# Grouping the modulation blocks that TensorE sums inside the layers of a two-network kernel

## The chip, the cores and the metric

The kernel runs on one core of a Trainium2 chip. The metric is the device time of one execution in microseconds, as the median of several runs. All times below are from the kernel's runs and from one profiled execution of it.

## What is computed

Two small networks run one after the other on 256 tokens of 2048 channels. Each has two layers, and each layer scales, shifts and gates its input by a modulation vector that comes from a conditioning vector and a large matrix. Cut to what matters here:

```python
def first_block(x, c, norm_g, w_ada, b_ada, w_in, ...):
    c_act = silu(c)
    for l in range(2):
        mod = c_act @ w_ada[l] + b_ada[l]          # (2048) @ (2048, 6144)
        shift, scale, gate = split(mod, 3)
        h = rmsnorm(x, norm_g[l]) * (1 + scale) + shift
        z = h @ w_in[l]                            # (256, 2048) @ (2048, 13 * 512)
        # four mixers on the 13 pieces of z: Fourier, neighbourhood attention,
        # retention, convolution; each times silu of its gate piece
        y = concat(mixers) @ w_out[l]              # (256, 2048) @ (2048, 2048)
        x = x + gate * y
    return rmsnorm(x, final_g)

def second_block(x, c, ctx, c_ctx, ada_w, ada_b, ...):   # a pool layer, then a latent attention layer
    for i in range(2):
        shift, scale, gate = split(silu(c) @ ada_w[i] + ada_b[i], 3)
        shift_c, scale_c, gate_c = split(silu(c_ctx) @ ada_w[i] + ada_b[i], 3)
        ...
```

The four modulation matrices (`ada_w` in the kernel, 50 MB each in float32) are read once, in blocks of 128 rows by 1024 columns, 512 KB each. 16 such blocks, one per 128 rows, make one piece of 1024 modulation values.

## The kernel before, in words

**Slots and steps.** Every large weight matrix comes in slots of 128 x 1024 values. SyncE loads a slot into `w_raw`, ScalarE copies it into `wh` (L1604), VectorE makes the remainder `wl` (L2413), and TensorE does three float32r products with it (`mm3`, L821 to L823). `w_raw`, `wh` and `wl` are rings of `RING = 4` slots: ScalarE may write slot g only when TensorE has used slot g-4 (`w_used`), and SyncE may load into it when VectorE has made `wl` of slot g-4 (`w_lo`). Four slots make a step t; a layer has `STEPS = 35` steps: 26 of the input product, one of two small products, eight of the output product. At the start of a step TensorE does what the mixers need of it (`mixers`), then the four slots i = 0 to 3. Ahead of slots 1, 2 and 3 it calls `ada_middle(t, i)`.

**Modulation blocks.** While the layers of the first network run, 192 blocks of later modulation pieces are summed. `ADA_DVE` and `ADA_PE` list how many blocks of which piece each step takes on VectorE and on TensorE; `ada_schedule()` turns both into one order, `ADA_SEQ`, in which the blocks of a step on the two engines alternate, VectorE's first. GpSimd issues the loads of `ADA_SEQ` strictly in that order (`ada_load`, L761), into a ring of `ADA_RING_A = 4` buffers (three of `ada_raw` and `ada_fourth`): the load of block q first waits until block q-4 has been used, by `ada_pe` if TensorE used it and by `ada_used` if VectorE did. VectorE uses a block in `ada_in_layer` by one multiply-add of 128 x 1024 (L2306), in the steps 8 to 25 mostly right after `wl` of the step's fourth slot. TensorE uses a block in `ada_slot` (L877): four float32 products with a 32-column operand, one for each quarter of the array's columns, which the profile shows as eight matmuls; then `ada_pe` rises by one. TensorE waits for the block's landing (`ada_here(q)`) just ahead of it.

**Where TensorE takes them.** In `ada_middle` a step with one or two TensorE blocks takes them all ahead of its third slot (i = 2). A step with three or four takes the first two ahead of the second slot (i = 1) and the others ahead of the fourth (i = 3). `ADA_PE` gives three blocks or four to 20 of the 46 steps that have any:

```python
ADA_PE = [{**spread(2, 4, [1, 2, 2, 2, 3, 3, 3]), **spread(4, 12, [4] + [3] * 4), **spread(5, 19, [2] * 8)},
          {**spread(2, 2, [2, 2, 2, 2, 2, 3, 3]), **spread(3, 11, [3] * 4 + [2] * 2), **spread(4, 18, [3] * 2 + [2] * 5),
           **spread(5, 26, [3, 4, 1, 2, 3, 3])}]
```

So in the first layer these are the steps 8, 9, 10 and 12 to 16 (step 12 has four blocks), in the second layer the steps 7, 8, 11 to 14, 18, 19, 26, 27, 30 and 31 (step 27 has four). No step with a finished piece (`ADA_FIN`) has three.

Of the kernel before, what the change touches and what calls it, by code (L numbers as in the profile page):

```python
# [107 lines left out]
ADA_FIN = [{11: 2, 17: 4, 18: 0, 27: 5, 28: 1, 34: 3}, {9: 2, 10: 0, 17: 3, 25: 4, 28: 1, 32: 5}]  # L108
# [11 lines left out]
def ada_schedule():  # L120

    slots, pe, dve, done = [], ADA_EARLY, 0, {}
    for l in range(DEPTH):
        for t in range(STEPS):
            if t in ADA_FIN[l] and ADA_FIN[l][t] in ADA_SUMMED[l]:
                pe += 1
                done[l, t] = pe
            elif t in ADA_FIN[l]:
                done[l, t] = pe
            a, b = (x[l].get(t, []) for x in (ADA_DVE, ADA_PE))  # L130
            for i in range(max(len(a), len(b))):
                if i < len(a):
                    dve += 1
                    slots.append((l, t, *a[i], False, dve))
                if i < len(b):
                    pe += 1
                    slots.append((l, t, *b[i], True, pe))
    return slots, done


ADA_SEQ, ADA_DONE = ada_schedule()
# [7 lines left out]
def ada_event(l, t):  # L149

    return 4 + l * 6 + sorted(ADA_FIN[l]).index(t)
# [157 lines left out]
def program(nc, x, w_in, w_small, w_out, ada_w, cols_d, rel_d, tab_d, ctx_in, pool_in, pool_grp, pool_out, mla_in,  # L309
# [4 lines left out]
    with ExitStack() as ctx:  # L314
# [220 lines left out]
        def ada_buf(r):  # L535
            return ada_raw[:, r, :] if r < ADA_RING else ada_fourth[:, :]

        def ada_here(q):

            if q < len(ADA_SEQ):  # L540
                return ada_landed[q % ADA_RING_A], 16 * (q // ADA_RING_A + 1)
            m = q - len(ADA_SEQ)
            return ada_landed[m % ADA_RING], 16 * (len(ADA_SEQ) // ADA_RING_A + m // ADA_RING + 1)
# [274 lines left out]
        def _(pe):  # L818
# [55 lines left out]
            def ada_slot(buf, k, bank_, first=0, last=ADA_SLOTS - 1):  # L874

                for q in range(4):
                    mm = pe.matmul(ps[32 * q:32 * q + 32, bank_, 0:256], cpad[:, k, :], buf[:, q * 256:(q + 1) * 256],  # L877
                                   start=k == first, stop=k == last, tile_position=(0, 32 * q),
                                   skip_group_check=True)
                mm.then_inc(ada_pe, 1)  # L880
# [9 lines left out]
            def ada_turn(event, bank_):  # L890

                pe.wait_ge(ada_row, event + 5 if event else 1)
                for h in range(2):
                    mm = pe.transpose(ps[:, bank_, 256 + h * P:256 + (h + 1) * P], ada_rows[:, h * P:(h + 1) * P], ident)
                mm.then_inc(ada_cols, 1)
# [33 lines left out]
            for l in range(DEPTH):  # L929
# [144 lines left out]
                def ada_middle(t, i):  # L1074

                    if i == 2 and t in ADA_FIN[l]:
                        ada_turn(ada_event(l, t), ADA_FIN_BANKS[l][t])
                    here = sum(x[4] and x[0:2] == (l, t) for x in ADA_SEQ)
                    seen = 0
                    for q, (layer, step, j, k, by_pe, _) in enumerate(ADA_SEQ):  # L1080
                        if by_pe and (layer, step) == (l, t):
                            seen += 1
                            if i != (2 if here < 3 else 1 if seen < 3 and t not in ADA_FIN[l] else 3):
                                continue
                            if k == 0:
                                pe.wait_ge(ada_read, max([4 + 6 * l] + [ada_event(l, x) + 1 for x in ADA_FIN[l] if x < t]))
                            pe.wait_ge(*ada_here(q))
                            ada_slot(ada_buf(q % ADA_RING_A), k, ADA_BANKS[l][t])

                for t in range(2 * NP_):  # L1090
                    ada_first(t)
                    mixers(t)
                    for i in range(RING):
                        g = t * RING + i
                        p, s = SLOTS_OF[l][g]
                        bank0 = 4 if l == 0 and p == 2 else 2 * (p % 2)
                        if i == 2:
                            channels(t)
                        if (t, i) == (SMALL_STEP - 1, 3):
                            turn_gate(0)  # L1100
                        if i:
                            ada_middle(t, i)
                        if p == 0:
                            pe.wait_ge(h_lo, l * 8 + s + 1)
                            if l and s == 0:
                                pe.wait_ge(ht_ok, l * 8 + 2)
                        if l and p == 1 and s == 0:
                            pe.wait_ge(ht_ok, l * 8 + 8)
                        if s == 0 and (p >= 2 if l else p >= 3):
                            pe.wait_ge(piece_out, l * NP_ + p - 1)  # L1110
                        slot(g, l * SLOTS_A + g, PIECES[p][2], bank0, SLOT_K * s, s == 0, s == BLK - 1, hh, hl)
                        if l == 0 and g < len(EARLY_AFTER):
                            if g == 8:
                                ada_turn(2, 6)
                            early_slots(2 * ADA_SLOTS + (EARLY_AFTER[g - 1] if g else 0), 2 * ADA_SLOTS + EARLY_AFTER[g])
                            if g + 1 == len(EARLY_AFTER):
                                ada_turn(3, 7)
# [4 lines left out]
                for i in range(RING):  # L1122
                    g = SMALL_STEP * RING + i
                    m, s = i // 2, i % 2
                    if i == 0:
                        pe.wait_ge(ft_lo, l * NCH + NCH)
                    if i:
                        ada_middle(SMALL_STEP, i)
                    if i == 2:
                        pe.wait_ge(t_row, 4 * l + 2)  # L1130
                        pe.wait_ge(cv_lo, l + 1)
                        pe.wait_ge(rt_var, l * 4 + 4)
                    slot(g, l * SLOTS_A + g, True, 4 if m else 2, SLOT_K * s, s == 0, s == 1,
                         chunks(sh if m else yh), chunks(sl if m else yl), 1 + m)
# [15 lines left out]
                for q in range(4):  # L1150
                    ada_first(OUT_STEP + 2 * q)
                    if q == 0:
                        pe.wait_ge(piece_out, l * NP_ + 13)
                    elif q == 1:
                        pe.wait_ge(small_mul, l * 4 + 2)
                    else:
                        pe.wait_ge(res_ok, l * 4 + q - 1)
                    for i in range(BLK):
                        g = (OUT_STEP + 2 * q) * RING + i
                        s = OUT_ORDER[i]  # L1160
                        if i == RING:
                            ada_first(OUT_STEP + 2 * q + 1)
                            if q == 1:
                                turn_gate(1)
                        if l and (2 * q + i // RING, i % RING) in CTX_TURN:
                            turn_ctx(CTX_TURN[2 * q + i // RING, i % RING])
                        if i % RING:
                            ada_middle(OUT_STEP + 2 * q + i // RING, i % RING)
                        if q == 0:
                            pe.wait_ge(o_lo, l * 8 + i + 1)  # L1170
                        slot(g, l * SLOTS_A + g, False, 2 * (q % 2), SLOT_K * s, i == 0, i == BLK - 1, hh, hl)
# [2126 lines left out]
```

## Time and profile before

| | |
|---|---|
| median of 3 runs | 2161.24 us (2158.2 to 2162.18) |
| the profiled execution | 2157.21 us, of which the span is 2155.4 us |
| TensorE matmul busy | 2087.6 us, 97% |
| TensorE weight loads | 1762.3 us, 82% |
| VectorE | 1513.2 us, 70% |
| ScalarE | 948.2 us, 44% |
| GpSimd | 201.7 us, 9% |
| chain that ended last, by engine | PE 70%, DVE 7%, DMA 4%, ACT 2%, issue 1% |
| modulation blocks loaded in the layers (L761) | 192 of 512 KB |

In the rows PE is TensorE, DVE is VectorE, ACT is ScalarE, POOL is GpSimd and SP is SyncE; L877 is line 877 of the kernel. Matmuls are pipelined, so the time that one more of them costs is the distance from start to start, not the duration shown. The first layer's steps run from about 60 to 560 us of the span, the second's to about 1050 us.

### The profile page before, as it was taken

The numbers are of one execution on the slowest core, as the hardware profiler recorded it, in microseconds if no ns is written. First come the engines' busy times: TensorE is split into PE (matmuls) and PEld (weight loads), VectorE is DVE, ScalarE is ACT, GpSimd is POOL, SyncE is SP. The second block draws the span as 40 slices with busy tenths as digits, with TensorE's granted clock in tenths as the row PEclk, the third lists the DMA queues.
The fourth block names the chain that finished last, engine by engine and source line by source line (L and its number), as shares of the span: only waits on it lengthen the run. The fifth ranks groups of instructions, "written<-read, shape, count | busy, mean of one in ns | idle before, by whom it ended". The sixth has DMA issues, their size and how long they took to land.

```text
span 2155.4 us, 32744 instructions
## 1 busy us (share of the span) xinstructions
PE 2087.6 (97%) x13530; PEld 1762.3 (82%) x13530; DVE 1513.2 (70%) x1923; ACT 948.2 (44%) x1318; POOL 201.7 (9%) x386
## 2 busy tenths in 40 slices
PE   5889999999999999999999999999999999999997
PEld 3668878887889878886987878787778999988876
DVE  0355879886765888865897868678788886455554
ACT  2234555553535555555632222223247553444452
POOL 2211110110011111110010100000100000000000
PEclk9999999999999999999999999999999999999999
DMA  9998887779697787777576646555887778322253
GB/s 381 383 332 304 276 315 245 251 270 343 201 356 265 263 274 264 256 270 275 184 275 201 212 146 196 163 174 166 299 289 256 233 255 265 103 70 77 78 191 131
DMA packets 215484, 511.40 MB, mean 237 GB/s; under 512 B 19728, under 2 KB 26096, under 8 KB 213680
## 3 DMA queue, kind: packets, MB, share of 16 engines
q1 hardware_dynamic: 155536, 297.83, 40.8%
q0 software_dynamic: 54464, 201.76, 26.9%
q10 hardware_dynamic: 5344, 9.84, 1.5%
q8 instruction: 101, 1.65, 0.3%
q14 instruction: 39, 0.32, 0.0%
HBM read 500.93 MB, written 8.43 MB: 236 GB/s over the span
## 4 chain that ended last, share of the span: by engine, by line
PE 70%; DVE 7%; DMA 4%; ACT 2%; issue 1%; DVEq 0%; ACTq 0%
PE ps L821 21%; PE ps L822 20%; PE ps L823 20%; DMA w_raw<-in_w_out 3%; DVE ada_acc L2306 2%; PE ps L877 2%; PE ps L1500 1%; DVE wl L2406 1%; DVE wl L2413 1%; PE ps L1492 1%; ACT wh L1604 1%; PE ps L1483 1%; DMA ada_raw<-in_ada_w 0%; PE ps L1199 0%; PE ps L1019 0%
## 5 line engine op out<-in xcount | busy, mean ns | idle before, releaser
L2413 DVE TENSOR_TENSOR wl<-w_raw,wh 128x1024 fp32r<-128x1024 f32 x280 | 334.7, 1221 | 197.9 <-ACT wh L1604 197.1
L1604 ACT ACTIVATE wh<-w_raw 128x1024 fp32r<-128x1024 f32 x280 | 291.6, 1056 | 346.9 <-PE ps L823 234.4
L1656 ACT ACTIVATE wh<-w_raw 128x1024 fp32r<-128x1024 f32 x220 | 230.5, 1057 | 403.2 <-PE ps L823 346.9
L821 PE MATMUL ps<-hh,wh 128*128 128x256 f32 x1280 | 371.5, 290 | 9.8 <-DVE hl L2474 9.0
L822 PE MATMUL ps<-hh,wl 128*128 128x256 f32 x1280 | 361.2, 282 | 0.0
L823 PE MATMUL ps<-hl,wh 128*128 128x256 f32 x1280 | 360.7, 282 | 0.0
L2406 DVE TENSOR_TENSOR wl<-w_raw,wh 128x1024 fp32r<-128x1024 f32 x220 | 266.8, 1221 | 130.6 <-ACT wh L1656 130.2
L821 PE MATMUL ps<-act_hl,wh 128*128 128x256 f32 (+1 forms) x1056 | 351.4, 333 | 2.9 <-DVE wl L2406 2.9
L822 PE MATMUL ps<-act_hl,wl 128*128 128x256 f32 (+1 forms) x1056 | 348.6, 330 | 0.0
L823 PE MATMUL ps<-act_hl,wh 128*128 128x256 f32 (+1 forms) x1056 | 348.4, 330 | 0.0
L2306 DVE SCALAR_TENSOR_TENSOR ada_acc<-ada_raw,cpad,ada_acc 128x1024 f32<-128x1024 f32 x263 | 329.5, 1280 | 13.5 <-DMA ada_raw<-in_ada_w 11.7
L821 PEld LDWEIGHTS ps<-hh,wh 128*128 128x128 f32 x1280 | 242.7, 190 | 36.3 <-issue 22.5
L822 PEld LDWEIGHTS ps<-hh,wl 128*128 128x128 f32 x1280 | 242.8, 190 | 0.4
L823 PEld LDWEIGHTS ps<-hl,wh 128*128 128x128 f32 x1280 | 243.0, 190 | 0.0
L821 PEld LDWEIGHTS ps<-act_hl,wh 128*128 128x128 f32 x1056 | 199.2, 189 | 24.9 <-issue 3.7
L822 PEld LDWEIGHTS ps<-act_hl,wl 128*128 128x128 f32 x1056 | 199.2, 189 | 21.0 <-issue 0.8
L823 PEld LDWEIGHTS ps<-act_hl,wh 128*128 128x128 f32 x1056 | 199.3, 189 | 20.3
L821 PE MATMUL ps<-wh,hh 128*128 128x512 f32 x448 | 183.4, 409 | 7.1 <-DVE wl L2413 7.1
L822 PE MATMUL ps<-wh,hl 128*128 128x512 f32 x448 | 178.1, 398 | 0.0
L823 PE MATMUL ps<-wl,hh 128*128 128x512 f32 x448 | 177.9, 397 | 0.0
L821 PE MATMUL ps<-wh,act_hl 128*128 128x512 f32 x384 | 154.8, 403 | 0.8 <-DVE wl L2406 0.7
L822 PE MATMUL ps<-wh,act_hl 128*128 128x512 f32 x384 | 151.8, 395 | 0.0
(414 smaller groups left out, 3113.0 us busy)
## 6 DMA issues: line engine op xcount, KB each, us to landing
ada_raw<-in_ada_w POOLq DMA_DIRECT2D x272, 512.0 KB, 5.3
w_raw<-in_w_in SPq DMA_DIRECT2D x208, 512.0 KB, 5.3
w_raw<-in_pool_in SPq DMA_DIRECT2D x72, 512.0 KB, 4.7
w_raw<-in_w_out SPq DMA_DIRECT2D x64, 512.0 KB, 7.6
w_raw<-in_mla_in SPq DMA_DIRECT2D x56, 512.0 KB, 4.8
ada_fourth<-in_ada_w POOLq DMA_DIRECT2D x48, 512.0 KB, 6.6
w_raw<-in_pool_out SPq DMA_DIRECT2D x48, 512.0 KB, 5.5
w_raw<-in_mla_out SPq DMA_DIRECT2D x32, 512.0 KB, 3.8
```

The lines of the kernel that those rows point to most:

```text
L821: pe.matmul(dst, ah, bh, start=start, stop=False, skip_group_check=True)
L822: pe.matmul(dst, al, bh, start=False, stop=False, skip_group_check=True)
L823: return pe.matmul(dst, ah, bl, start=False, stop=stop, skip_group_check=True)
L877: mm = pe.matmul(ps[32 * q:32 * q + 32, bank_, 0:256], cpad[:, k, :], buf[:, q * 256:(q + 1) * 256], start=k == first, stop=k == last, til ...
L1483: mm = pe.matmul(ps[:, 2 + 2 * h + i, :], q[lo:lo + 64, 512 + i * P:512 + (i + 1) * P], k[lo:lo + 64, :], start=False, stop=j == 2, skip_g ...
L1492: mm = pe.transpose(ps[:, bank0 + kt // 2, (kt % 2) * SEQ + i * P:(kt % 2) * SEQ + (i + 1) * P], pm[:, h, i * 512 + kt * P:i * 512 + (kt + ...
L1500: mm = pe.matmul(ps[:, 0, off:off + SEQ], vb[:, b, kt * 256 + h * VD:kt * 256 + (h + 1) * VD], ptm[:, h, kt * SEQ:(kt + 1) * SEQ], start=k ...
L1604: act.activation(wh[:, g % RING, :], w_raw[:, g % RING, :], ACT.Copy).then_inc(w_hi, 1)
L1656: act.activation(as_raw(g, wh[:, r, :]), raw_of(g), ACT.Copy).then_inc(w_hi, 1)
L2306: ins = dve.scalar_tensor_tensor(ada_acc[:, v, :], buf, csil(i, k), ada_acc[:, v, :], ALU.mult, ALU.add)
L2406: dve.tensor_tensor(as_raw(g, wl[:, r, :]), raw_of(g), as_raw(g, wh[:, r, :].bitcast(F32)), ALU.subtract).then_inc(w_lo, 1)
L2413: dve.tensor_tensor(wl[:, g % RING, :], w_raw[:, g % RING, :], wh[:, g % RING, :].bitcast(F32), ALU.subtract).then_inc(w_lo, 1)
```

## The change

The condition on i in `ada_middle` becomes the same for every step: whatever a step has of TensorE's blocks stands in one group ahead of its third slot. `ADA_SEQ`, the order of the loads, the rings and VectorE's part are untouched.

```diff
                     if i == 2 and t in ADA_FIN[l]:
                         ada_turn(ada_event(l, t), ADA_FIN_BANKS[l][t])
-                    here = sum(x[4] and x[0:2] == (l, t) for x in ADA_SEQ)
-                    seen = 0
                     for q, (layer, step, j, k, by_pe, _) in enumerate(ADA_SEQ):
                         if by_pe and (layer, step) == (l, t):
-                            seen += 1
-                            if i != (2 if here < 3 else 1 if seen < 3 and t not in ADA_FIN[l] else 3):
+                            if i != 2:
                                 continue
```

## Rows read from the trace of the kernel before

**Rows 1.** Waits of TensorE, 118 to 1015 us: total, times, longest.
```profile
PE ps L821 <- DVE wl L2413: 7.1, 5, 3.0
...
PE ps L1019 <- DVE yl L2620: 0.4, 1, 0.4
```

**Rows 2.** Timeline of VectorE, step 10: start, duration, instruction, idle time before it.
```profile
221.81 1.23 DVE L2413 TENSOR_TENSOR wl<-w_raw,wh 128x1024 fp32r<-128x1024 f32 x1 [2.01 <-ACT wh L1604]
```

**Rows 3.** Timeline of TensorE: groups of two, one and three blocks (eight matmuls each).
```profile
194.27 0.28 PE L823 MATMUL ps<-hl,wh 128*128 128x256 f32 x1
194.48 1.07 PE L877 MATMUL ps<-ada_raw,cpad 128*32 128x256 f32 x16
195.48 0.39 PE L821 MATMUL ps<-hh,wh 128*128 128x256 f32 x1
...
201.03 0.28 PE L822 MATMUL ps<-hh,wl 128*128 128x256 f32 x1
201.14 0.27 PE L823 MATMUL ps<-hl,wh 128*128 128x256 f32 x1
201.35 0.64 PE L877 MATMUL ps<-ada_fourth,cpad 128*32 128x256 f32 x8
201.92 0.39 PE L821 MATMUL ps<-hh,wh 128*128 128x256 f32 x1
...
81.08 0.27 PE L823 MATMUL ps<-hl,wh 128*128 128x256 f32 x1
81.29 1.50 PE L877 MATMUL ps<-xb,cpad 128*32 128x256 f32 x24
82.72 0.38 PE L821 MATMUL ps<-hh,wh 128*128 128x256 f32 x1
```

**Rows 4.** TensorE: first block of steps 10, 12, 14; of step 8, second layer.
```profile
224.27 0.42 PE L877 MATMUL ps<-ada_raw,cpad 128*32 128x256 f32 x4
...
252.29 0.42 PE L877 MATMUL ps<-ada_fourth,cpad 128*32 128x256 f32 x4
...
282.71 0.42 PE L877 MATMUL ps<-ada_raw,cpad 128*32 128x256 f32 x4
...
674.32 0.42 PE L877 MATMUL ps<-ada_raw,cpad 128*32 128x256 f32 x4
```

**Rows 5.** Timeline of GpSimd, the third blocks' loads of these steps and of step 8.
```profile
194.74 0.53 POOL L761 DMA_DIRECT2D ada_fourth<-in_ada_w  x1 [6.96 <-DVE ada_acc L2306]
...
224.53 0.53 POOL L761 DMA_DIRECT2D ada_raw<-in_ada_w  x1 [6.09 <-DVE ada_acc L2306]
...
252.56 0.53 POOL L761 DMA_DIRECT2D ada_raw<-in_ada_w  x1 [13.31 <-DVE ada_acc L2306]
...
283.01 0.53 POOL L761 DMA_DIRECT2D ada_raw<-in_ada_w  x1 [6.09 <-DVE ada_acc L2306]
...
667.96 0.53 POOL L761 DMA_DIRECT2D ada_raw<-in_ada_w  x1 [1.12 <-PE ps L877]
```

**Rows 6.** DMA issues at 194.7, 224.5, 252.6, 283.0, 311.4 us: KB, us to landing.
```profile
ada_fourth<-in_ada_w POOLq DMA_DIRECT2D x1, 512.0 KB, 6.0
...
ada_raw<-in_ada_w POOLq DMA_DIRECT2D x1, 512.0 KB, 6.3
...
ada_raw<-in_ada_w POOLq DMA_DIRECT2D x1, 512.0 KB, 5.9
...
ada_raw<-in_ada_w POOLq DMA_DIRECT2D x1, 512.0 KB, 5.4
...
ada_raw<-in_ada_w POOLq DMA_DIRECT2D x1, 512.0 KB, 4.5
```

**Rows 7.** The 188 loads of L761 from 118 to 1015 us, to landing.
```profile
DMA to landing us min/median/max: 4.0/5.9/13.8
```

**Rows 8.** TensorE after an idle time, and its granted clock behind it.
```profile
566.02 1.22 PE L937 MATMUL ps<-dec,ones 128*128 128x256 f32 x2 [2.70 <-DVE dec L2513]
...
566.10:569.40 3.30, 3.30 (x14) 3.01 (x14) 1.60 (x4) 1.08 (x3) 0.00 (x0) 0.50 0.00 0
```

## The prediction

> **What bounds the kernel now.** I read the page's first part, then the waits of TensorE in the layers, then the timelines of TensorE, GpSimd and VectorE around the steps that the change touches. The page has TensorE busy for 97% of the span. In the 897 us from 118 to 1015 us its waits fill eight rows, from 7.1 us down to 0.4 [rows 1], all behind VectorE or ScalarE or of plain issue; none is for a modulation block. So in the layers TensorE sets the end: what its queue gets shorter or longer by, the span does too. VectorE and ScalarE wait for it, through the ring of four slots: ahead of a step's fourth `wl`, VectorE was idle for 2.01 us behind ScalarE's `wh` [rows 2], which itself waits for TensorE to free the slot. That matters below: VectorE's modulation block of a step comes right behind this `wl`, so a delay of TensorE delays it by as much, and the buffer that it frees too.
>
> **Term 1, the switches that go.** From the start of the last matmul ahead of a group to the start of the first one behind it take 1.21 us for two blocks (195.48 - 194.27), 0.78 for one (201.92 - 201.14) and 1.64 for three (82.72 - 81.08), and 0.11 to 0.12 where no group stands between [rows 3]. So a block costs 0.43, and going to the small shape and back costs what is left: two groups of 2 and 1 take 1.99, one group of 3 takes 1.64 and leaves one plain distance of 0.12: 0.23 saved. The TensorEngine Tiling (Array Packing) page of the Trainium skill, under Key Properties, says that a change of the tiling mode drains TensorE. The rows agree with it in sign, but the price they show is only this 0.23. 20 steps lose one switch pair, two of them with 2 and 2 blocks, for which the same difference holds: 20 x 0.23 = 4.6 us saved. The bounds are narrow, since the rows show all three group sizes: 4 to 5 us.
>
> **Term 2, when the third block is wanted.** This is what the change moves. Call T1 the start of a step's first block today, ahead of its second slot. Two slots take 5.77 us (195.48 to 201.14, and one distance) [rows 3], 2.9 each. With one group, the first block starts at T1 + 2.9, the second 0.43 later and the third at T1 + 2.9 + 0.9 = T1 + 3.8. Today it starts at 201.35 with T1 = 194.48 [rows 3], T1 + 6.9. So the third block is wanted 3.1 us earlier, while the first two release their buffers 2.9 us later. TensorE's queue is in order: if the block has not landed, the third and fourth slot of the step stand behind the wait, and ScalarE (`wh` of the next step) behind them.
>
> Where does the third block's load begin? Blocks are loaded in one order through four buffers. In steps 8, 10, 14 and 16 of the first layer it takes the buffer of a VectorE block that is used at about T1: the loads issue at 194.74, 224.53 and 283.01, each released by `ada_acc` [rows 5], against T1 of 194.48, 224.27 and 282.71 [rows 3, 4]. The change doesn't move VectorE's block against TensorE, so issue and T1 keep their distance. The landings are 6.0, 6.3, 5.4 and, in step 16, 4.5 us behind the issue [rows 6]. The waits that arise:
> - step 8: 194.74 + 6.0 - (194.48 + 3.8) = 2.5
> - step 10: 224.53 + 6.3 - (224.27 + 3.8) = 2.8
> - step 14: 283.01 + 5.4 - (282.71 + 3.8) = 1.9
> - step 16: landing 4.5, issued within 0.3 us of T1 as in the others, against 3.8: 0.7 (0.4 to 1.0).
>
> Step 12 has four TensorE blocks and is the worst. Its third is issued at 252.56 and lands 5.9 later, at 258.5; it is wanted at 252.29 + 3.8 = 256.1: 2.4 us [rows 4 to 6]. Its fourth takes the buffer of the step's own first block, which now stands in the same group. That block starts at 255.2 and ends 0.6 later (the duration of one block [rows 3]); the issue comes about 0.3 behind it, at 256.1. Its landing is not in the trace of before; I take the median of all the loads, 5.9 [rows 7], because it meets the same traffic as the others: 262.0. TensorE is done with the third at 258.9, so it waits 3.1 us more. It waits about 0.2 us there today. The other 14 merged steps have room: the tightest of those that I looked at, step 8 of the second layer, issues its third at 667.96 for T1 = 674.32 [rows 4, 5], 10.2 us before it will be wanted. Step 27 there has four blocks too, but with no VectorE block between them its fourth takes a buffer of the step before. The same goes for VectorE's blocks that follow: they get buffers up to 2.9 us later and are used a step later, which costs nothing as long as a load stays near its 6 us.
>
> Sum of the waits: 2.5 + 2.8 + 1.9 + 0.7 + 2.4 + 3.1 - 0.2 = 13.2 us. Bounds: with every landing at the quickest of the 188, 4.0 us [rows 7], the five single ones are 0.5 each but 0.2 in step 16, and the fourth block 3.1: 5.3 - 0.2 = 5.1. The upper end is the sum itself with 0.5 us more for each landing, since after a group three buffers come free at once: 16. I take 13.2, because five of the six landings are those of the very loads.
>
> **Term 3, the clock.** After an idle time of 2.70 us TensorE ran at a granted clock of 0.50, its lower level of 1.2 GHz, for 3.3 us and somewhat more [rows 8], where busy stretches show the upper one. That costs half of it, 1.7 us. Waits of 2.4 to 3.1 us are new in steps 8, 10 and 12; whether each is followed by such a stretch the trace can't tell. I take two: 3.4 us. Bounds: none, and all six, 10.2.
>
> **What is removed besides.** The counting at build time costs nothing on the chip. No instruction is added; matmuls, transfers and their order stay as they are. SP's queue isn't moved past anything, and POOL's keeps its order, but stands behind a wait that now ends later.
>
> **Sum.** 13.2 + 3.4 - 4.6 = +12.0 us. Against the profiled execution, 2157.21 us, this gives 2169.2; the median shown is 4.0 above that execution, so the forecast for it is 2161.2 + 12.0 = **2173.2 us**. 0.2% of the time, 4.3 us, is about what a measurement of this kernel can tell from no change.
>
> **Rivals.**
> 1. *The loads land in time* (not slower). The first term stands, and the late loads arrive as the quickest row, 4.0 us behind their issue, so that only the fourth block of step 12 is really late: 5.1 - 4.6 = +0.5, 2161.7 us. It decides at 3.8 us behind the issue. For it: while TensorE waits, fewer weight slots are asked for, so these loads share less. Against it: 4.0 is the minimum of 188, and four of the five rows are at 5.4 or more. The DMA: Bandwidth & Descriptors page of the Trainium skill, in its Anatomy of one DMA, gives 2.0 us plus bytes over 436e3 for a load from this queue. For 512 KB that is an estimate of 3.2 us, by which all but the fourth block of step 12 would be in time and the sum about -2.0, 2159.2 us. No row of this trace reaches it. Chance 0.15.
> 2. *The waits are given back later.* VectorE and ScalarE get time while TensorE stands, and those waits of TensorE behind VectorE that come after step 16, 2.70 us the longest [rows 8], shrink. I price them at 7 us, what the largest row of waits holds [rows 1], which gives 12.0 - 7 = +5, 2166.2 us. Against it: the ring lets VectorE run no more than four slots ahead, and it is mostly there already. Chance 0.10.
> 3. *The clock falls after each wait* and the loads bunch: 16 + 10.2 - 4.6 = +21.6 at the most, some 2180 us as its middle. Chance 0.12.
> 4. *The full saving*: all loads in time, step 12 too, -4.6, 2156.6 us. It would need the fourth block's load to be over before its own buffer's first user has ended. Chance 0.03.
>
> **How the numbers follow.** The forecast's own case, 2167 to 2178 us, has the remaining 0.60. The range has to leave out 0.2: I leave out rivals 1 and 4 (0.18) and the tail of 3, which gives 2163.5 to 2179.5. Faster by over 0.2% is rival 4, 0.03. Within 0.2% is rival 1 but for a little, 0.14. Slower by over 0.2% is the rest, 0.83.
>
> **What would show it.** In the profile of the changed kernel, the waits of TensorE must have rows for the transfers of `ada_raw` and `ada_fourth`, some 13 us in six waits, none in the second layer; the timeline must show groups of 24 matmuls of 1.5 us, and in step 12 one broken twice; the load of that step's fourth block must be released by L877 at about T1 + 3.8. The clock must be at 0.50 behind one to three of these waits. Distance from start to start across a group of three must be 1.64. The prediction is wrong if those waits are under 5 us together, if VectorE waits for blocks as well, or if later waits shrink by what these add.

## The result: 0.29% slower, and the profile after

The changed kernel takes 2166.55 us (median of 9 runs, 2164.26 to 2169.67) against 2160.84 us for the kernel before (9 runs). The ratio of the two is 1.0029, with a 95% interval of 1.0021 to 1.0038: +6.3 us, between 4.5 and 8.2 (the medians themselves are 5.7 apart; below, too, differences in us are worked out from the ratios). The forecast was 2173.2 us, +12.0. The sign, the place and the mechanism were right, and the size was twice what was measured.

The profiled execution after took 2165.60 us, its span 2163.8. The waits of TensorE in the layers, which in the first profile before named no modulation block, now do (118 to 1025 us; total, times, longest):

```profile
PE ps L821 <- DVE wl L2410: 5.9, 3, 3.0
PE ps L877 <- DMA ada_raw<-in_ada_w: 5.0, 4, 1.9
PE ps L877 <- DMA ada_fourth<-in_ada_w: 4.9, 3, 2.7
```

The timeline of TensorE of the same kernel, in the steps 8, 10, 12, 14 and 16 of the first layer, shows six of the seven waits for a block; the seventh, 0.35 us at 649 us, is in the second layer, in a step that the change doesn't touch (start, duration, instruction, idle time before it):

```profile
200.11 0.28 PE L823 MATMUL ps<-hl,wh 128*128 128x256 f32 x1
200.32 1.07 PE L877 MATMUL ps<-ada_raw,cpad 128*32 128x256 f32 x16
204.13 0.64 PE L877 MATMUL ps<-ada_fourth,cpad 128*32 128x256 f32 x8 [2.74 <-DMA ada_fourth<-in_ada_w]
204.70 0.39 PE L821 MATMUL ps<-hh,wh 128*128 128x256 f32 x1
...
236.21 0.64 PE L877 MATMUL ps<-ada_raw,cpad 128*32 128x256 f32 x8 [1.23 <-DMA ada_raw<-in_ada_w]
...
263.06 0.64 PE L877 MATMUL ps<-ada_fourth,cpad 128*32 128x256 f32 x8
263.51 0.61 PE L877 MATMUL ps<-ada_raw,cpad 128*32 128x256 f32 x8
266.00 0.64 PE L877 MATMUL ps<-ada_raw,cpad 128*32 128x256 f32 x8 [1.87 <-DMA ada_raw<-in_ada_w]
268.45 1.08 PE L877 MATMUL ps<-ada_fourth,cpad 128*32 128x256 f32 x8 [1.82 <-DMA ada_fourth<-in_ada_w]
269.46 0.58 PE L821 MATMUL ps<-hh,wh 128*128 128x256 f32 x1
...
301.19 0.64 PE L877 MATMUL ps<-ada_raw,cpad 128*32 128x256 f32 x8 [1.19 <-DMA ada_raw<-in_ada_w]
...
330.15 0.64 PE L877 MATMUL ps<-ada_raw,cpad 128*32 128x256 f32 x8 [0.69 <-DMA ada_raw<-in_ada_w]
```

These are the six waits of the forecast, in its five steps: the third block in each, and the fourth in step 12. Step 12's group is broken twice. VectorE waits for blocks no more than before (0.8 us in one wait before, 1.1 in one after). Where no block is late, a group of three takes 1.65 us from start to start, as here in the second layer (732.86 - 731.21), and the prediction asked for 1.64:

```profile
731.21 0.28 PE L823 MATMUL ps<-hl,wh 128*128 128x256 f32 x1
...
732.86 0.39 PE L821 MATMUL ps<-hh,wh 128*128 128x256 f32 x1
```

GpSimd's timeline shows the reuse inside that group: the load of the fourth block goes out 0.3 us behind the end of the group's first block (263.06 + 0.64). That is 3.8 us behind T1, the start that the step's first block had in the old order. In the kernel before, the first block stood ahead of the second slot, and this load went out at 253.26, 1.0 us behind T1.

```profile
260.48 0.53 POOL L761 DMA_DIRECT2D ada_raw<-in_ada_w  x1 [13.32 <-DVE ada_acc L2303]
264.02 0.53 POOL L761 DMA_DIRECT2D ada_fourth<-in_ada_w  x1 [3.02 <-PE ps L877]
```

A load's landing is in the DMA issues. Against 6.0, 6.3, 5.9, 5.4 and 4.5 before [rows 6], the same five third blocks took 6.3, 4.8, 5.5, 4.7 and 4.6 us. The shorter ones of the steps 10 and 14 are no chance of one execution: in the four profiles with their groups ahead of the third slot and VectorE's part untouched (both of the changed kernel, e3 and e6 below) step 10's load takes 4.6 to 5.1 us, in the five with the old grouping there 5.5 to 6.5; in step 14 it is 4.3 to 5.1 against 4.9 to 5.6. In the old order three more blocks' loads go out 0.7 to 1.8 us behind it, in the new one only from 3.5 us behind it on. Whether that is the reason was not separated, and in step 8, where the order of events is the same, the landing didn't get shorter.

Behind the waits of the steps 8 and 12 the clock fell to its lower level, 0.50, for 3.3 us and for two such stretches in a row (windows; the third figure from the right is the granted clock):

```profile
205.40:208.70 3.30, 3.30 (x18) 3.30 (x17) 0.00 (x0) 0.00 (x0) 0.23 (x1) 0.50 0.95 312
266.90:273.50 6.60, 5.05 (x27) 4.24 (x28) 5.63 (x11) 0.00 (x0) 1.06 (x2) 0.50 0.96 353
```

**Where the time goes, step by step.** TensorE's first weight matmul of a step has a start time in each timeline. The difference of these between two kernels, and how it grows over a step, is a finer measure than the medians: from step 8 to 16 the two profiles before agree to some hundredths of a microsecond, but for 0.3 in step 12. Ahead of step 8 the kernels lie up to 3.3 us apart, by waits behind VectorE that differ from one execution to the next, and from step 17 to the second layer they differ again. Only the growth within a stretch counts. The table has, for each kernel (the other rows are the experiments below), what steps 8, 10, 12, 14 and 16 of the first layer cost in us against the first profile before, then three longer stretches.

| kernel | 8 | 10 | 12 | 14 | 16 | steps 8 to 16 | step 17 to second layer's 6 | second layer's 7 to 27 |
|---|---|---|---|---|---|---|---|---|
| before again | 0.00 | 0.00 | 0.31 | 0.00 | 0.00 | +0.3 | 0.0 | 0.0 |
| changed | 4.14 | 1.11 | 5.82 | 1.07 | 0.57 | +11.7 | -2.4 | -3.35 |
| changed, again | 3.81 | 1.38 | 5.00 | 0.64 | 0.91 | +10.7 | +2.2 | -3.33 |
| e1 fourth slot | -0.33 | 0.48 | 5.94 | 0.67 | -0.33 | +5.4 | +1.2 | -3.33 |
| e2 second layer | 0.00 | 0.00 | 0.39 | 0.00 | 0.00 | +0.4 | +0.6 | -3.35 |
| e3 five late | 3.67 | 0.90 | 5.38 | 1.45 | 0.67 | +12.1 | +0.5 | 0.0 |
| e4 fourth but 12 | -0.33 | 0.39 | -0.04 | 0.69 | -0.34 | -0.7 | +0.4 | -3.35 |
| e5 vector earlier | 0.79 | -0.28 | 5.84 | -0.34 | -0.15 | +4.8 | +3.7 | -3.35 |
| e6 split 12 | 3.64 | 1.18 | 0.09 | 0.97 | 0.90 | +5.8 | -1.8 | -3.35 |
| e7 more switches | 0.00 | 0.00 | 0.11 | 0.00 | 0.00 | +0.1 | +4.8 | +2.17 |
| e8 fifteen | 0.00 | 0.00 | 0.13 | 0.00 | 0.01 | -0.9 | -1.2 | -3.31 |
| e9 vector first | 0.97 | 0.07 | 1.97 | -0.35 | -0.34 | +1.3 | +1.9 | -3.35 |

The steps 9, 13 and 15 of the first layer read -0.33 to -0.35 in every kernel that merges them. So does each of the ten merged steps in the last column: ten of them make -3.31 to -3.35 in eight kernels. That is the saving of one merge, 0.34 us, where nothing is late.

### The profile page after: what moved, and what is told of

Read it like the earlier page. It is cut to its first block, busy times and chain, and to the rows that moved or that the text cites. A ratio compares the mean times of both kernels' runs of the same rounds, so it can differ in the third digit from the quotient of the medians.

```text
span 2163.8 us, 32744 instructions
## 1 busy us (share of the span) xinstructions
PE 2081.7 (96%) x13530; PEld 1762.0 (81%) x13530; DVE 1513.2 (70%) x1923; ACT 948.7 (44%) x1318; POOL 201.6 (9%) x386
## 3 DMA queue, kind: packets, MB, share of 16 engines
q8 instruction: 101, 1.65, 0.3%
## 4 chain that ended last, share of the span: by engine, by line
PE 71%; DVE 7%; DMA 2%; ACT 2%; issue 1%; POOL 0%; DVEq 0%; ACTq 0%
PE ps L821 21%; PE ps L822 21%; PE ps L823 21%; DVE ada_acc L2303 2%; PE ps L877 2%; PE ps L1497 1%; DVE wl L2403 1%; DMA ada_raw<-in_ada_w 1%; DMA w_raw<-in_w_out 1%; PE ps L1489 1%; PE ps L1480 1%; DMA w_raw<-in_pool_out 0%; DVE wl L2410 0%; DMA ada_fourth<-in_ada_w 0%; ACT wh L1653 0%
## 5 line engine op out<-in xcount | busy, mean ns | idle before, releaser
L821 PE MATMUL ps<-hh,wh 128*128 128x256 f32 x1280 | 372.0, 291 | 11.4 <-DVE hl L2471 9.4
L821 PE MATMUL ps<-act_hl,wh 128*128 128x256 f32 (+1 forms) x1056 | 350.6, 332 | 3.4 <-DVE wl L2403 3.4
L821 PEld LDWEIGHTS ps<-hh,wh 128*128 128x128 f32 x1280 | 244.8, 191 | 33.5 <-issue 19.9
L821 PEld LDWEIGHTS ps<-act_hl,wh 128*128 128x128 f32 x1056 | 198.6, 188 | 25.1 <-issue 3.4
L821 PE MATMUL ps<-wh,hh 128*128 128x512 f32 x448 | 181.7, 405 | 5.9 <-DVE wl L2410 5.9
L821 PE MATMUL ps<-wh,act_hl 128*128 128x512 f32 x384 | 154.8, 403 | 2.3 <-DVE wl L2403 2.2
```

Source lines behind the costliest of these rows:

```text
L821: pe.matmul(dst, ah, bh, start=start, stop=False, skip_group_check=True)
```

## The experiments

The theory (A): the third block is wanted 3.1 us earlier, and its load, which waits for a buffer that VectorE frees at about T1, comes too late; in step 12 the fourth block also waits for its own group's first. The rivals: (B) bunching, that a group frees three buffers at once and the loads behind it come slower; (C) traffic, that the loads land late because the merged group shifts the weight loads into them; and that waits are given back later. All runs are compared with the kernel before on the same chip.

**e1, the group ahead of the fourth slot.**

```diff
-                            if i != (2 if here < 3 else 1 if seen < 3 and t not in ADA_FIN[l] else 3):
+                            if i != (2 if here < 3 else 3):
```

> All of a step's blocks in one group, as in the changed kernel, but ahead of the fourth slot where a step has three or four (20 steps). Theory A (late loads: the change loses time because the third block is wanted 3.1 us earlier): the third blocks are wanted at about the time at which they were wanted before, so the waits of steps 8, 10, 14 and 16 of the first layer go, and only the fourth block of step 12 waits, since it still takes the buffer of its own group's first block: some 4.2 us and one stretch of low clock, 1.7 us. With 20 x 0.34 = 6.8 us of switches saved: -0.9 us against the kernel before, 2160. Theory B (bunching: what costs is that a group frees three buffers at once and the loads behind it come in a bunch): the loads bunch here too, the waits stay near the changed kernel's 11 us, and the time is some 6 us above before.

Measured: 2162.74 us against 2161.21; ratio 1.0004 (0.9994 to 1.0013), +0.9 us. Steps 8 and 16 lose their waits and save their switch, as A has it; step 12 keeps its cost (5.94 against 5.82). But in steps 10 and 14 TensorE still waits 0.6 and 0.8 us for the third block, which A had excluded. So B is wrong as the main cause; whether it has a small part, the landings in e4 leave open.

**e4, the same, with step 12 left in two groups.**

```diff
+                            if i != (2 if here < 3 else 3 if (l, t) != (0, 12) else
+                                     1 if seen < 3 and t not in ADA_FIN[l] else 3):
```

> As the kernel with the group ahead of the fourth slot, but step 12 of the first layer keeps its two groups of two. Theory A: no block is late anywhere, 19 x 0.34 = 6.5 us saved, 2154.5 us, better than both kernels. Theory B: waits as in the changed kernel outside step 12, and no gain.

Measured: 2157.56 us against 2161.21; ratio 0.9982 (0.9971 to 0.9992), -3.9 us where -6.5 was expected. Step 12's cost is gone (-0.04). The two waits of 0.8 and less are those of steps 10 and 14 again. GpSimd's timeline and the landing of the load that is late, in step 10:

```profile
218.03 0.53 POOL L761 DMA_DIRECT2D ada_fourth<-in_ada_w  x1
224.46 0.53 POOL L761 DMA_DIRECT2D ada_raw<-in_ada_w  x1 [5.90 <-DVE ada_acc L2306]
```
```profile
ada_raw<-in_ada_w POOLq DMA_DIRECT2D x1, 512.0 KB, 7.0
```

It goes out at the same place as before, but takes 7.0 us where it took 6.3 [rows 6], and 7.1 in step 14, where it took 5.4; e1 has 7.0 and 7.1 too. Here the loads ahead of it went out at 217 to 218 us, because the buffers of step 9 come free 5.8 us later; the last of them landed 0.8 us behind the late load's issue. Whether it is they that hold it up, or the weight loads beside it, was not separated.

**e2, the change in the second layer alone.**

```diff
+                            if i != (2 if here < 3 or l else 1 if seen < 3 and t not in ADA_FIN[l] else 3):
```

> The change in the second layer alone (12 of the 20 steps); the first layer is grouped as before. Theory A: no load is late there, so 12 x 0.34 = 4.1 us are saved, 2156.8 us. By the prediction's 0.23 a switch it would be 2.8 us, 2158. Theory B: the same bunching as in the first layer should cost something here, and the kernel is at or above the time of before.

Measured: 2157.09 us against 2161.21; ratio 0.9980 (0.9971 to 0.9989), -4.3 us. Twelve merges at 0.34 are 4.1, and at the prediction's 0.23 they are 2.8; the interval, 2.4 to 6.3 us saved, holds both, and only the steps' -0.34 each tell them apart. B, which has every merged group cost something, falls here. A wait of 0.4 us at 641 us is in an unmerged step: such waits for a block, 0.3 to 1.0 us in steps of either layer that a kernel leaves alone, come in seven of the 13 profiles at 465 to 652 us, in the old grouping too (e7), and go in the others.

**e3, the change in the five late steps alone.**

```diff
+                            if i != (2 if here < 3 or (not l and t in (8, 10, 12, 14, 16)) else
+                                     1 if seen < 3 and t not in ADA_FIN[l] else 3):
```

> The change in the five steps with late loads alone (8, 10, 12, 14, 16 of the first layer). Theory A: waits of 11.0 us net of today's 0.2 and about two stretches of low clock, 3.1 us, less 5 x 0.34 = 1.7 us: +12.4 us, 2173. If later waits give part of it back, as between the two layers in the changed kernel's profile (2.9 us), +9.5, 2170. Theory B (bunching over all steps): no more than the changed kernel's own +5.7.

Measured: 2174.72 us against 2161.21; ratio 1.0057 (1.0044 to 1.0070), +12.3 us, and +12.1 in the table. A quarter of the merged steps costs twice what the whole change does; the other fifteen pay half of it back. It is also the clearest answer to the rival that the waits are given back later: of the 12.1 us lost in the steps 8 to 16, the whole program still shows 12.3 (9.5 to 15.1).

**e8, the fifteen steps without a late load.**

```diff
+                            if i != (2 if here < 3 or l or t in (9, 13, 15) else
+                                     1 if seen < 3 and t not in ADA_FIN[l] else 3):
```

> The change in the 15 steps without a late load: all twelve of the second layer and 9, 13 and 15 of the first. Theory A: 15 x 0.34 = 5.1 us saved and no new wait, 2156.1 us, the best of the versions with the group ahead of the third slot. Theory B (bunching costs something wherever a group of three frees its buffers at once): less than the 4.1 us of the second layer alone.

Measured: 2155.12 us against 2161.44; ratio 0.9973 (0.9963 to 0.9982), -5.8 us. It is faster than both kernels, and the lowest ratio of all those tried. In its waits between 180 and 350 us one row for a block is left, in a step that is grouped as before:

```profile
PE ps L877 <- DMA ada_fourth<-in_ada_w: 0.2, 1, 0.2
```

e3 and e8 together, +12.3 and -5.8, make +6.5: the change's own +6.3. Each of the two has an interval of 2 to 3 us to either side, so the medians alone could hide as much. The table says the same from the steps: 12.1 - 0.9 = 11.2 us in the steps 8 to 16, where the changed kernel's two profiles have 11.7 and 10.7.

**e6, the changed kernel with step 12 left in two groups.**

```diff
-                            if i != 2:
+                            if i != (2 if here < 3 or (l, t) != (0, 12) else
+                                     1 if seen < 3 and t not in ADA_FIN[l] else 3):
```

> The changed kernel, but step 12 of the first layer keeps its two groups of two. Step 12 is there the costliest: 4.55 us of waiting and about 1.6 of low clock in the profile of the changed kernel. Theory A: 19 x 0.34 = 6.5 us saved; waits 2.95, 1.44, 1.40 and 0.90 in the other four, 1.5 us of low clock behind step 8: 6.5 to 8.2, so +1.0 us against before, 2162, and some 5 us under the changed kernel. Rival: if the time that TensorE loses there were given back by later waits, splitting step 12 would gain less than 3 us.

Measured: 2162.52 us against 2161.44; ratio 1.0010 (0.9998 to 1.0021), +2.2 us: about 4 us under the changed kernel (6.3 - 2.2), by ratios with intervals of some 2 us each. The table gives 5.8 less 0.1 for the step itself. This run doesn't exclude the rival that puts the gain under 3 us: the ratios are too coarse, and giving back would show in the stretch behind step 16, where the executions differ by several us anyway. What speaks against it is e3.

**e5, VectorE's block one slot earlier.** Only VectorE's order changes, in the five late steps: its modulation blocks stand ahead of `wl` of the fourth slot.

```diff
                 for t in range(STEPS):
                     for i in range(RING):
+                        if i == 3 and not l and t in (8, 10, 12, 14, 16):
+                            ada_in_layer(t)
                         if t >= EARLY_STEPS[l]:
                             lo(t, i, base)
...
-                    if t in ADA_AHEAD:
+                    if t in ADA_AHEAD and (l or t not in (8, 10, 12, 14, 16)):
                         ada_in_layer(t)
```

> The changed kernel, but in the steps 8, 10, 12, 14 and 16 of the first layer VectorE takes its modulation blocks ahead of wl of the step's fourth slot and not behind it, so that it frees their buffers about 2.9 us earlier against TensorE. Nothing of TensorE's order differs from the changed kernel. Theory A (the third block's load starts too late because VectorE frees its buffer at T1): the waits of steps 8, 10, 14 and 16 go or fall under 0.5 us, and in step 12 the third block's wait goes while the fourth's stays at about 4 us with a stretch of low clock behind it. Sum against before: 20 x 0.34 = 6.8 saved, 4.0 + 1.7 - 0.2 lost, some -1 us, 2160. Theory C (the waits come of traffic: the loads land late because TensorE's merged group shifts the weight loads into them): an earlier issue does not change the landing by as much, waits of over 1 us stay in each of the five steps, and the time is above 2163.

Measured: 2162.01 us against 2161.44; ratio 1.0004 (0.9994 to 1.0013), +0.9 us. The waits of the steps 10, 14 and 16 are gone from the list (16 still costs 0.2 more than a free merge), and step 8 falls from 4.14 to 0.79, with a wait of 0.9 us where at most 0.5 was expected. This shows the cause directly for these four: TensorE's instructions and the loads' order are those of the changed kernel, and what was moved is the point at which VectorE frees the buffer. Their loads went out 2.7 to 2.8 us earlier against T1, but landed only 0.7 to 1.8 us earlier, since they took 7.2, 6.3, 6.0 and 6.7 us in place of 6.3, 4.8, 4.7 and 4.6. So C is wrong in what it forecast for the waits, and right in that a load's landing time moves with its issue. Step 12 stays at 5.84, with one wait in place of two:

```profile
255.60 1.12 PE L877 MATMUL ps<-ada_raw,cpad 128*32 128x256 f32 x16
260.50 1.08 PE L877 MATMUL ps<-ada_fourth,cpad 128*32 128x256 f32 x8 [3.77 <-DMA ada_fourth<-in_ada_w]
```

The third block is in time now, and nothing is gained: the fourth's load starts when the first block ends, whatever the third does. Its wait holds the third's in it.

**e9, and VectorE's blocks first in the order of step 12.** As e5, and `ada_schedule()` puts both VectorE blocks of step 12 ahead of the four of TensorE, so that no block of the group takes a buffer of the group.

```diff
+            if (l, t) == (0, 12):
+                for x in a:
+                    dve += 1
+                    slots.append((l, t, *x, False, dve))
+                a = []
             for i in range(max(len(a), len(b))):
```

> As the kernel in which VectorE takes its blocks one slot earlier, and in step 12 of the first layer the order of the loads is changed too: VectorE's two blocks first, then TensorE's four. So the fourth TensorE block takes the buffer of VectorE's second block and no longer that of the first block of its own group. Theory A (step 12's cost is this reuse inside the group): the third's load can issue about T1 - 2.6 and the fourth's about 1.3 later, both land near the time at which they are wanted, T1 + 3.8 and T1 + 4.3: a wait of at most 1 us in place of 4.5, and no stretch of low clock. The drift of step 12 against before falls from +5.8 to between -0.3 and +0.7, and the whole is 5 us faster than before, 2156. Rival (four blocks in one group are what costs, by the order on TensorE or the traffic): step 12 keeps a wait of 3 us or more.

Measured: 2160.01 us against 2160.50; ratio 0.9998 (0.9986 to 1.0011), no difference that can be told, where about -5 us was expected. Step 12 falls from 5.84 to 1.97: its two waits are 1.30 and 0.82 us, and no low clock follows. So the reuse inside the group was the larger part of step 12's cost. The expectation, +0.7 at the most for that step, was missed, because both loads took 6.4 and 6.5 us and went out 1.4 us later against T1 than I had reckoned (1.2 us ahead of it and 0.1 behind it, not 2.6 and 1.3 ahead). That is 1.3 us or more of the miss, and step 8, at 0.97 where -0.34 would be a free merge, is another 1.3; the rest can't be told from the spread. The two waits of step 12:

```profile
260.44 0.64 PE L882 MATMUL ps<-ada_raw,cpad 128*32 128x256 f32 x8 [1.30 <-DMA ada_raw<-in_ada_w]
261.90 0.64 PE L882 MATMUL ps<-ada_fourth,cpad 128*32 128x256 f32 x8 [0.82 <-DMA ada_fourth<-in_ada_w]
```

**e7, more switches.** The opposite of the change, in 16 steps with two blocks.

```diff
+                            if i != (1 + seen if here == 2 and (t >= 19 or l and t >= 15) else
+                                     2 if here < 3 else 1 if seen < 3 and t not in ADA_FIN[l] else 3):
```

> The dose of the switch alone, the other way round: the kernel before, but 16 steps with two TensorE blocks (19 to 26 of the first layer; 15, 16, 20 to 24 and 29 of the second) take one ahead of the third slot and the other ahead of the fourth. No block is wanted earlier. At 0.34 us a switch pair, as the drift from step to step in the changed kernel shows: +5.4 us, 2166.6. At the prediction's 0.23: +3.7, 2164.9.

Measured: 2165.42 us against 2161.44; ratio 1.0018 (1.0007 to 1.0028), +3.9 us. The interval holds both sizes. The steps of the one profile tell more: eleven of the 16 grow by 0.31 to 0.35 us, two by 0.18, and three (19 and 25 of the first layer, 29 of the second) by nothing; the 16 add up to 3.9 us. Step 29's 0.34 goes into a wait behind `wl` that follows it, 2.33 us before and 1.84 here; for the steps 19 and 25 I didn't look for the reason. None shows 0.23, and the merges of the other kernels show 0.34 wherever nothing is late. The timeline says where the missing 0.11 is. The first weight matmul behind a group is followed 0.22 us later, where 0.12 is usual:

```profile
392.29 0.27 PE L823 MATMUL ps<-hl,wh 128*128 128x256 f32 x1
392.49 0.64 PE L877 MATMUL ps<-ada_raw,cpad 128*32 128x256 f32 x8
393.06 0.39 PE L821 MATMUL ps<-hh,wh 128*128 128x256 f32 x1
393.28 0.28 PE L822 MATMUL ps<-hh,wl 128*128 128x256 f32 x1
```

**Both kernels once more, unchanged.**

> The kernel before, unchanged, for a second profile. In the first one TensorE waits behind VectorE at 150, 539, 549, 563, 570 and 983 us. If these waits are the same from run to run, the time given back between the two layers in the changed kernel's profile (2.9 us) is an effect of the change. If they differ by one to three us in this run too, it is not.

> The changed kernel, unchanged, for a second profile. The waits for blocks in the steps 8, 10, 12, 14 and 16 of the first layer should repeat within some 0.5 us each (2.95, 1.44, 4.55, 1.40, 0.90), since they hang on fixed distances and on landings of 4.4 to 6.4 us; the waits behind VectorE's wl outside these steps may differ by one to three us.

Measured, one run each: 2158.85 and 2166.36 us. The kernel before repeats its waits between the layers closely in its two profiles. The changed one doesn't: from step 17 to the second layer's step 6 it gains 2.4 us in one profile and loses 2.2 in the other. Its waits between 500 and 650 us, in the first profile and then in the second:

```profile
PE ps L937 <- DVE dec L2510: 2.2, 1, 2.2
PE ps L821 <- DVE hl L2462: 2.0, 1, 2.0
PE ps L877 <- DMA ada_fourth<-in_ada_w: 0.4, 1, 0.4
```
```profile
PE ps L937 <- DVE dec L2510: 2.6, 1, 2.6
PE ps L821 <- DVE wl L2410: 2.2, 4, 0.7
PE ps L821 <- DVE hl L2462: 2.0, 1, 2.0
```

So the 2.9 us that seemed to be given back between the layers belong to that execution and can't be put down to the change: four waits behind `wl` were absent in it and are there in the other. Over all the profiles this stretch lies between -2.4 and +3.7 (e7's +4.8 has 1.8 of its own switches in it). The idle times of the five steps repeat to 0.1 to 0.4 us. What the steps cost repeats less well, to 0.3 to 0.8: in step 12 the idle times are the same to 0.1, and the cost is 5.82 in one profile and 5.00 in the other.

## Why the forecast was right, and where its size was off

- **What bounds the kernel** was right: TensorE's queue in the layers. The second layer's merges alone (e2) come out at the end of the program, 4.3 us for twelve (2.4 to 6.3), as the sum of what each saves in its step (4.1).
- **The switch (term 1)** was mis-sized: "0.23 saved" is 0.34. I measured to the start of the first matmul behind a group, and the switch's cost goes on for one matmul more. The trace of before had it: the first L821 behind each group lasts 0.39 or 0.38 us where others last 0.28 [rows 3], and I read past that. 20 merges save 6.8 us and not 4.6, so this is 2.2 us of the miss. The trace agrees in sign with the drain at a change of tiling mode that the Trainium skill's page TensorEngine Tiling (Array Packing) states under Key Properties; a price is in the rows alone.
- **When the third block is wanted, and where its load begins (term 2)** was right in each of the five steps, and no sixth merged step waited anew (the 0.35 us at 649 us is in a step that isn't touched, and is missing in the second profile). The size: 13.2 us forecast. From start to start across a group I read 4.59 us in step 8 (204.70 - 200.11) and 3.08 in step 10, 1.64 being the undisturbed group of three, so 2.95 and 1.44; in the same way 1.40 in step 14 and 0.90 in step 16. In step 12 the third block starts 2.49 us behind the second and the fourth 2.45 behind the third, where 0.43 is usual: 2.1 and 2.0, together 4.1. That is 10.6 net of the 0.2 before. The step that failed in size is the landing: I took over the landings of the kernel before as fixed, "because five of the six landings are those of the very loads", and they moved with the change. Step 10 was put too high by 1.4 us and step 14 by 0.5, since their loads landed sooner than before; step 12 was put too high by 1.4, most of it in the fourth block, for which I took the median landing of 5.9 us and which took 4.4 (issue at 264.02, use at 268.45). Steps 8 and 16 were put too low by 0.5 and 0.2.
- **The clock (term 3)** came as taken: two of the waits were followed by a granted clock of 0.50, steps 8 and 12 in both profiles. What their steps lost beyond wait and switch is 1.5 us (4.14 + 0.34 - 2.95) and 2.3 (5.82 + 0.34 + 0.2 - 4.1), of which the fourth block of step 12 itself, 1.08 us long where 0.64 is usual, has 0.4: 3.8, with 3.4 forecast. That it would be two of the six was a guess, and it was lucky.
- **The sum** with these sizes is 10.6 + 3.8 - 6.8 = +7.6 us; the second profile gives +6.6 (10.7 in the steps 8 to 16, less 12 x 0.34 for the second layer). The measured +6.3 has both inside its interval, 4.5 to 8.2. So the waits (2.6 us too high), the switch (2.2 too small a saving) and the clock (0.4 too low) account for 4.4 of the 5.7 us of the miss, and the rest can't be told from the spread.
- **The rivals.** That all loads but one land in time didn't happen; the estimate of 3.2 us a load, from the Trainium skill's page DMA: Bandwidth & Descriptors (Anatomy of one DMA), is under every landing read here, 4.4 to 6.3 us for the six. In rival 1 the block is in time if it lands 3.5 us behind its issue and not 3.8: it is wanted at T1 + 3.8, and the issue comes 0.3 behind T1. The waits weren't given back later, as far as the spread lets one say (e3). The 7 us that I set as that rival's price were too much in any case: 3.0 of the 7.1 in that row of waits lie at 150 us, ahead of step 8. Nor did the clock fall after every wait. The full saving exists, but only where no load is late (e2 and e8).

## What to carry to other kernels

Before work is moved in an in-order queue, write down for each thing it needs when that is wanted after the move and which event starts its load; a merge that saves a fixed cost everywhere pays only where this slack is longer than a load. Where blocks go through a ring in one order, count how far a group reaches in that order, with the other engine's blocks in between. If it is further than the ring has buffers, its last block needs a buffer that the group itself frees, and that wait can't be hidden by loading earlier (step 12). And a landing time read in the kernel before isn't a constant: step 10's went from 6.3 to 4.8 us with the change, and back to 6.3 when its load was issued earlier (e5). When the price of a switch is read from a timeline, measure until the distances are the usual ones again, not until the first instruction behind it.

## What the hardware showed that was not expected

- The price of a group of small float32 matmuls between large float32r ones is 0.34 us beside its blocks, in groups of one to four of them (2 + 1 and 2 + 2 merged, 2 split into 1 + 1), and a third of it sits between the first and the second matmul behind the group.
- The length of an idle time alone doesn't say whether the clock falls. In the changed kernel's profile idle times of 2.74 us and of 1.87 and 1.82 in a row were followed by a granted clock of 0.50; one of 2.97 us, at 992 us, was not. In e5 idle times of 3.00 and 2.88 us were not either. So this term could be forecast only as a count.

```profile
995.20 0.50 PE L821 MATMUL ps<-wh,hh 128*128 128x512 f32 x1 [2.97 <-DVE wl L2410]
995.54 0.39 PE L822 MATMUL ps<-wh,hl 128*128 128x512 f32 x1
```

- One and the same load of 512 KB takes a different time in each version: the third block of step 14 took 5.4 us in the kernel before, 4.7 and 4.3 in the changed one, 6.0 in e5 and 7.1 in e4. Why, no run here separates. An average over all loads is no price for one that TensorE stands and waits for.
